# One transformer-like layer on one core: slicing the S5 outputs between projection tiles and reordering the attention heads

## The chip, the cores and the metric

The kernel runs on one core of one Trainium2 chip. TensorE (PE) does matrix products and transposes into eight PSUM banks, VectorE (DVE) and ScalarE (ACT) work on SBUF and PSUM, GpSimd (Pool) on SBUF alone, and SyncE (SP) issues most of the DMAs. The metric is device time in microseconds, from several runs, lower is better.

## The reference

One layer over 512 tokens of width 1024, batch 1, in float32, with a memory of 256 rows:

```
proj = rms_norm(h) @ w_in                # u_ssm, q, k, v: 512 columns each
y_ssm = s5_mixer(u_ssm, ...)             # 32 groups x 16 channels, 64 complex states, gelu, GLU
y_att = moba_attention(q, k, v, bias)    # 8 heads of 64; here plain causal attention with a T5 bias
h = h + concat(rms_norm(y_ssm), rms_norm(y_att)) @ w_out
h = h + memory_cross_attention(rms_norm(h), rms_norm(mem), ...)   # 4 heads of 128
h = h + conv_ffn(rms_norm(h), ...)       # width 2816, depthwise convolution of 3, silu gate
```

## The kernel before

Every engine has a program written out by hand, and its order is the order of the source; semaphores are the only tie between engines. A weight matrix is cut into units of 1024 columns per partition. Two units make a chunk of 1 MB, loaded by `load_chunk` (L451) into one of two `raw` buffers. ScalarE rounds a unit to fp32r in `split_hi` (L468), DVE takes the remainder in `split_lo` (L484), and both halves lie in a ring of four units, `wring`. A product is three matmuls, hi*hi, hi*lo and lo*hi (`mm3`, L503). A projection unit (`rows_unit`, L1713) goes over four token tiles with two steps of the depth, so it is 4 x 2 x 3 = 24 matmuls of 512 columns.

PSUM banks are handed out by `plan` (L268): `use(bank, name)` gives a name the next turn of a bank, `fill` (L343) makes TensorE wait until the earlier user of that bank is drained, and `drained` says that its last reader is done. So a name waits for the name that stands before it in the list of the same bank.

The S5 mixer runs in four quarters q of eight groups. TensorE transposes the input weights (`weights_in`), makes the input states (`states_in`, banks 4 and 5 as vr, vi) and the short kernels (`kernels_in`, banks 6 and 7 as ka, kb, laid out in Toeplitz form by eight DMAs in `t_load`, L599); DVE runs `scan(q)` (L1373) over vr, vi and drains them; TensorE then does `outputs(q)` (L1863), 24 small matmuls into banks 6 and 7 (ye, yo); ScalarE copies them out (`y_out`), SP carries them through DRAM (`y_back`, L611), and DVE adds the skip (`skip_in`). Between these steps stand the units of the q, k and v projections, 4 to 15. The PE order is at L1894 to L1916. `m_transposes` transposes the memory into banks 6, 7, 4, 5, read by ScalarE (`m_hi`) and drained by DVE (`m_lo`, L1363). `head_event` and `head_rows` are DVE's norms of q, k and mk per head; qt and kt are the transposed q and k, also in banks 6, 7, 4, 5. The roots of the row norms of x come from a pow on Pool and a correction of four steps on DVE (`root("x")`, L1207); TensorE needs them for the bank xb, behind the transposes cr and cm.

The attention runs over 32 steps s (four query tiles x eight heads): `scores(s)`, `logits(s)` on DVE, `probabilities(s)` (exp) on ScalarE, `prob_transposes(s)` into bank 6, `pt_evac(s)` in turns on ScalarE (even s, in its round s+1) and DVE (odd s, in its round s+1), `values(s)`. Scores use banks 3, 4, 5 in turn and are issued two steps ahead, first in a step. Other matrix work is laid between: memory keys (units 16 to 19) at `MK_AT`, GLU tiles at `GLU_AT`, memory values at `MV_AT`, the S5 half of the output projection in 16 pieces at `SOUT_AT`, whose inputs (the gated S5 result times its gain, hi part on ScalarE, lo part on DVE, strided) are made at s = 16 to 18. `SPLIT_AT` lays the splits over the steps. Behind the loop follow the attention half of the output projection, the memory attention and the feed-forward part, which take most of the time and are not changed but for the shape of the chunks of w_out.

Of the kernel before, what the change touches and what calls it, by code (L numbers as in the profile page):

```python
# [20 lines left out]
TT = T // 128  # L21
# [3 lines left out]
G, CG, NS = 32, 16, 64  # L25
GP = G // 2
# [28 lines left out]
U_SSM, U_Q, U_K, U_V, U_MK, U_GLU = 0, 4, 8, 12, 16, 20  # L55
U_MV, U_OUT, U_XQ, U_XO, U_UP, U_DOWN = 22, 26, 34, 38, 42, 86
# [13 lines left out]
SPLIT_AT = {2: 20, 4: 21, 6: 22, 8: 23, 11: 24, 13: 25, 15: 26, 17: 27, 19: 28, 21: 29, 30: 30, 31: 31}  # L70
YA_AT = [13, 23, 26]
# [27 lines left out]
def layer(nc, A, out):  # L99
# [10 lines left out]
    with ctx:  # L110
# [48 lines left out]
        turn_at = [region(at, GP, NC) for at in (R0 + 1152, R0 + 3328)]  # L159
# [36 lines left out]
        w1p = [region(at, 2, 512) for at in (R0 + 2304, R2 + 2048, R2 + 3072, R1 + 4096)]  # L196
        qT = region(R2, 4, T)
# [70 lines left out]
        def plan():  # L268
# [53 lines left out]
            for b in range(8):  # L322
# [6 lines left out]
                     U_GLU: "z1", U_GLU + 1: "z3", U_OUT + 1: "g30", U_OUT + 3: "g31",  # L329
                     U_OA + 1: "o30", U_OA + 3: "o31", U_XQ + 3: "qx3", U_XO + 1: "w30", U_XO + 3: "w31"})  # L330
# [69 lines left out]
        def chunk_src(c, r=0):  # L400
# [1816 lines left out]
```

## Time and profile before

| | |
|---|---|
| median of three runs (lowest, highest) | 746.7 us (744.6, 746.76) |
| the profiled execution | 746.4 us |
| its span, first to last instruction | 744.8 us |
| TensorE busy, share of the span | 97% |
| DVE, ScalarE, Pool busy | 57%, 42%, 15% |
| mean granted TensorE clock | 0.977 |

TensorE's busy time is modelled, so it says where the engine stood idle but not how fast it went; the granted clock is shown beside it, 1.00 being 2.4 GHz and 0.50 being 1.2 GHz. A line number can be that of a helper, so operations are told apart by their tiles: `pb` are the PSUM banks, `xs` and `bs` the inputs in two parts, `wring` the split weights, `F` one large buffer that holds nearly all else.

### The profile page before, as it was taken

To read this page: it belongs to the slowest core of one execution; us is meant where nothing else is said; L and a number is where in the kernel's file an instruction comes from. 1 tells how busy PE (TensorE), PEld (TensorE's weight loads), DVE (VectorE), ACT (ScalarE), POOL (GpSimd) and SP (SyncE) were. 2 spreads that over 40 slices of the span, in tenths; PEclk is the share of its full clock that TensorE was granted. 3 is DMA by queue.
4 is the path that set the end of the run, shared out by engine and by line. 5 is a ranking of instruction groups with operands and counts; after the bars stand their busy time and mean duration, and the time that the engine had idled before them with its cause. 6 is when DMAs were issued, how large, how long until landed. Compare 5 with 4: busy or idle time off the path is not lost.

```text
span 744.8 us, 10611 instructions
## 1 busy us (share of the span) xinstructions
PE 720.0 (97%) x3809; PEld 600.0 (81%) x3809; DVE 423.5 (57%) x718; ACT 312.1 (42%) x523; POOL 108.5 (15%) x114
## 2 busy tenths in 40 slices
PE   8798999988999999999999999999999999999998
PEld 8777888876777787787899888888888887888886
DVE  5989948144775445768586555555555474333322
ACT  5632746336674333535355434333343442323220
POOL 3889922004020000110010000000000000000000
PEclk9999999879998999999999999999999999999999
DMA  8637313266313003303031333233223213322302
GB/s 252 197 104 140 102 73 89 83 194 213 119 56 114 1 1 142 113 1 113 1 114 57 113 113 102 67 113 113 65 103 113 95 74 114 113 73 96 113 1 113
DMA packets 64022, 73.93 MB, mean 99 GB/s; under 512 B 20873, under 2 KB 47796, under 8 KB 63860
## 3 DMA queue, kind: packets, MB, share of 16 engines
q1 hardware_dynamic: 60196, 66.12, 27.6%
q10 hardware_dynamic: 3792, 7.36, 2.9%
q8 instruction: 21, 0.34, 0.2%
q14 instruction: 13, 0.11, 0.0%
HBM read 68.08 MB, written 5.78 MB: 99 GB/s over the span
## 4 chain that ended last, share of the span: by engine, by line
PE 87%; DVE 6%; ACT 3%; issue 2%; SPq 1%; DMA 1%; POOL 0%; ACTq 0%; DVEq 0%
PE pb L505 24%; PE pb L507 24%; PE pb L506 23%; PE pb L1690 11%; PE pb L1693 5%; DVE F L1189 2%; ACT F L833 1%; ACT xs L833 1%; DVE wring L491 1%; ACT wring L477 1%; DVE wring L488 1%; DVE xs L1195 1%; SPq L608 1%; ACT L833 1%; DVE F L1195 0%
## 5 line engine op out<-in xcount | busy, mean ns | idle before, releaser
L488 DVE TENSOR_TENSOR wring<-raw,wring 128x1024 fp32r<-128x1024 f32 x100 | 126.9, 1271 | 93.0 <-ACT wring L477 92.9
L505 PE MATMUL pb<-xs,wring 128*128 128x512 f32 (+1 forms) x448 | 166.0, 371 | 0.3 <-issue 0.2
L507 PE MATMUL pb<-xs,wring 128*128 128x512 f32 (+1 forms) x448 | 164.9, 368 | 0.0
L506 PE MATMUL pb<-xs,wring 128*128 128x512 f32 (+1 forms) x448 | 164.7, 368 | 0.0
L477 ACT ACTIVATE wring<-raw 128x1024 fp32r<-128x1024 f32 x100 | 105.2, 1055 | 105.0 <-PE pb L507 83.1
L1195 DVE SCALAR_TENSOR_TENSOR F<-pb,ccol,F 128x511 f32<-128x511 f32 x88 | 65.9, 749 | 103.3 <-ACT F L833 97.4
L505 PE MATMUL pb<-wring,bs 128*128 128x512 f32 x240 | 98.5, 410 | 0.9 <-DVE F L1195 0.5
L505 PEld LDWEIGHTS pb<-xs,wring 128*128 128x128 f32 x448 | 84.9, 190 | 14.8 <-issue 0.6
L506 PEld LDWEIGHTS pb<-xs,wring 128*128 128x128 f32 x448 | 84.9, 190 | 13.8
L507 PEld LDWEIGHTS pb<-xs,wring 128*128 128x128 f32 x448 | 84.8, 189 | 13.8
L507 PE MATMUL pb<-wring,bs 128*128 128x512 f32 x240 | 94.8, 395 | 0.0
L506 PE MATMUL pb<-wring,bs 128*128 128x512 f32 x240 | 94.7, 395 | 0.0
L1690 PE MATMUL pb<-F 128*128 128x64 f32 (+6 forms) x736 | 85.2, 290 | 3.4 <-DMA F<-F 2.4
L833 ACT ACTIVATE F<-pb,ccol 128x512 f32<-128x512 f32 x44 | 34.2, 778 | 121.4 <-PE pb L507 117.4
L505 PE MATMUL pb<-wring,xs 128*128 128x512 f32 x192 | 82.8, 431 | 1.4 <-DVE wring L491 0.9
L1690 PEld LDWEIGHTS pb<-F 128*128 128x128 f32 (+3 forms) x736 | 68.4, 175 | 9.8 <-DMA F<-F 2.9
L507 PE MATMUL pb<-wring,xs 128*128 128x512 f32 x192 | 76.1, 396 | 0.0
L506 PE MATMUL pb<-wring,xs 128*128 128x512 f32 x192 | 76.0, 396 | 0.0
L1693 PE MATMUL pb<-ident,F 128*128 128x128 f32 (+1 forms) x359 | 55.6, 282 | 11.7 <-ACT F L833 3.7
L1693 PEld LDWEIGHTS pb<-ident,F 128*128 128x128 f32 (+1 forms) x359 | 44.2, 145 | 25.1 <-issue 9.3
L505 PEld LDWEIGHTS pb<-wring,bs 128*128 128x128 f32 x240 | 46.1, 192 | 11.4 <-DVE F L1195 0.9
L507 PEld LDWEIGHTS pb<-wring,bs 128*128 128x128 f32 x240 | 45.8, 191 | 10.0
(138 smaller groups left out, 754.7 us busy)
## 6 DMA issues: line engine op xcount, KB each, us to landing
raw<-in_ffn_w_up SPq DMA_DIRECT2D x22, 1024.0 KB, 5.0
raw<-in_ffn_w_down SPq DMA_DIRECT2D x11, 1024.0 KB, 4.7
F<-in_x SPq DMA_DIRECT2D x8, 512.0 KB, 5.3
raw<-in_w_in ACTq DMA_DIRECT2D x4, 1024.0 KB, 5.7
raw<-in_w_out SPq DMA_DIRECT2D x4, 1024.0 KB, 5.0
raw<-in_w_in SPq DMA_DIRECT2D x3, 1024.0 KB, 6.3
raw<-in_x_wkv ACTq DMA_DIRECT2D x2, 1024.0 KB, 5.0
raw<-in_x_wkv SPq DMA_DIRECT2D x2, 1024.0 KB, 7.7
```

The costliest lines, as they stand in the source:

```text
L477: ins = nc.scalar.activation(w_unit(u, 0), raw_unit(u), ACT.Copy)
L488: ins = nc.vector.tensor_tensor(w_unit(u, 1), raw_unit(u), w_unit(u, 0).bitcast(f32), ALU.subtract)
L491: ins = nc.vector.scalar_tensor_tensor(out=w_unit(u, 1)[:, k, :], in0=raw_unit(u)[:, k, :], scalar=gcol[:, g + k:g + k + 1], in1=w_unit(u, ...
L505: nc.tensor.matmul(ps, lh, rh, start=first, stop=False)
L506: nc.tensor.matmul(ps, lh, rl_, start=False, stop=False)
L507: return nc.tensor.matmul(ps, ll, rh, start=False, stop=last)
L608: sync.dma_start(toep[d * CG:(d + 1) * CG, :, (L - 1 - d) * CG:], kt[0:CG, :, 0:(d + 1) * CG]).then_inc(t_in[q], 16)
L833: return nc.scalar.activation(o, i, f, **k)
L1189: return V.tensor_tensor(o, a, b, op)
L1195: return V.scalar_tensor_tensor(out=o, in0=a, scalar=s1, in1=b, op0=o1, op1=o2)
L1690: return nc.tensor.matmul(o, l, r, start=start, stop=stop)
L1693: return nc.tensor.transpose(o, i, ident[0:i.shape[0], 0:i.shape[0]])
```

## The change

The order of the programs on all engines is changed between the first projections and the end of the attention loop; the amount of matrix work stays.

- `rows_unit` becomes `rows_tile`, one token tile of a unit (six matmuls). `outputs(q)` becomes `outputs(q, a)`, a quarter of it. Slices of `outputs(0)`, `(1)`, `(2)` stand in turn with the tiles of units 8, 11, 14; those of `outputs(3)` with tiles of the last two memory key units, behind `scores(0)` and `scores(1)`.
- `kernels_in(q)` moves ahead of `states_in(q)` for q = 1, 2, 3, with `weights_in(q)`; two more projection units stand ahead of `m_transposes`. SP issues `t_load(q+1)` ahead of `y_back(q)`, and `scr_b` after the first.
- The memory keys move out of the head loop into the last S5 quarter. In the loop each step gets at most one tile of other work: memory values at s = 0 to 7, GLU at 8 to 11, output pieces at 14 to 30. Scores go to banks 3 and 4 only, behind the transposes of the step.
- The gated S5 parts are made one per step, on ScalarE at s = 11 to 14 and on DVE at s = 12 to 15. Chunks of w_out are two depth rows x 1024 columns.
- The correction of the roots of x moves from DVE to Pool, and DVE, ScalarE and SP are reordered to match.

The core of the diff (of the constants, the bank plan and each engine's order):

```diff
-U_SSM, U_Q, U_K, U_V, U_MK, U_GLU = 0, 4, 8, 12, 16, 20
-U_MV, U_OUT, U_XQ, U_XO, U_UP, U_DOWN = 22, 26, 34, 38, 42, 86
+U_SSM, U_Q, U_K, U_V, U_MK, U_MV = 0, 4, 8, 12, 16, 20
+U_GLU, U_OUT, U_XQ, U_XO, U_UP, U_DOWN = 24, 26, 34, 38, 42, 86
...
-MK_AT = [0, 2, 4, 6]
+MV_AT = [0, 1, 2, 3, 4, 5, 6, 7]
 GLU_AT = [8, 9, 10, 11]
-MV_AT = [12, 14, 16, 19]
+KX_AT = [5, 7]
+SS_AT = 17
-SOUT_AT = [23, 23, 24, 24, 25, 25, 26, 26, 27, 27, 28, 28, 29, 30, 31, 31]
+SOUT_AT = [14, 15, 16, 17, 18, 19, 21, 22, 23, 24, 25, 26, 27, 28, 29, 30]
+SOUT_ORDER = [(0, 1, 2, 3), (0, 2, 1, 3), (0, 2, 1, 3), (0, 2, 1, 3)]
+SOUT_DONE = [18, 19, 20, 23, 25, 27, 29, 31]
-SPLIT_AT = {2: 20, 4: 21, 6: 22, 8: 23, 11: 24, 13: 25, 15: 26, 17: 27, 19: 28, 21: 29, 30: 30, 31: 31}
-YA_AT = [13, 23, 26]
+SPLIT_AT = {0: 22, 1: 23, 2: 24, 4: 25, 11: 26, 12: 27, 13: 28, 15: 29, 28: 30, 30: 31}
+YA_AT = [12, 20, 26]
...
+                use(4, f"w1r{q}"); use(5, f"w1i{q}"); use(6, f"ka{q}"); use(7, f"kb{q}")
+                if q == 3:
+                    four("kt")
+                use(4, f"vr{q}"); use(5, f"vi{q}")
+                if q < 2:
+                    four(("m", "qt")[q])
                 use(6, f"ye{q}"); use(7, f"yo{q}")
             for s in range(TT * H):
-                use(3 + s % 3, f"sc{s}"); use(6, f"pt{s}")
+                use(3 + s % 2, f"sc{s}"); use(6, f"pt{s}")
...
@@ SyncE @@
+                t_load(q + 1)
                 y_back(q)
-                t_load(q + 1)
...
@@ Pool @@
             pow_event(EVN["x"])
+            pool.wait_ge(pow_ready, 1)
+            r, t, m = ev(rs, "x"), rt[:, 1, 0:TT], ev(ms, "x")
+            link(mul(t, r, r))
+            link(mul(t, t, m))
+            link(ts(t, t, -0.5, 1.5, ALU.mult, ALU.add))
+            mul(r, r, t).then_inc(xr_ready, 1)
...
+                if q == NQ - 1:
+                    pow_event(EVN["mk"])
...
@@ ScalarE @@
+            split_hi(act, 6)
             weights_in(0)
+            load_chunk(act, 4)
+            split_hi(act, 7)
+            kernels_in(0)
             act.wait_ge(turn_ready, 1)
             A_(ph[:, 1], turn_at[1], ACT.Sin, scale=-2 * math.pi)
...
             probabilities(0)
+            y_out(3)
+            act.wait_ge(mem_ready, 1)
+            mem_rows("mk", mkrow)
...
@@ DVE @@
             u_evac(2)
+            split_lo(dve, 5)
+            u_evac(3)
             turns(2)
-            u_evac(3)
+            split_lo(dve, 6)
             turns(3)
+            split_lo(dve, 7)
...
             scan(0)
+            split_lo(dve, 8)
+            split_lo(dve, 9)
+            head_event("q", qk, range(TT), H, "q")
+            m_lo()
+            split_lo(dve, 10)
+            head_rows("q", qk, range(TT), H, HD)
...
@@ TensorE @@
+            proj(4, U_Q, "q")
             weights_in(0)
+            proj(5, U_Q, "q")
+            states_in(0)
+            kernels_in(0)
+            proj(6, U_Q, "q")
+            proj(7, U_Q, "q")
             m_transposes()
+            for t in range(TT):
+                outputs(0, t)
+                proj_tile(8, U_K, "k", t)
             weights_in(1)
+            kernels_in(1)
             proj(9, U_K, "k")
+            states_in(1)
             proj(10, U_K, "k")
+            for t in range(TT):
+                head_transposes("qt", 0, qk, t)
+            for t in range(TT):
+                outputs(1, t)
+                proj_tile(11, U_K, "k", t)
             weights_in(2)
+            kernels_in(2)
             proj(12, U_V, "v")
+            states_in(2)
             proj(13, U_V, "v")
+            for t in range(TT):
+                outputs(2, t)
+                proj_tile(14, U_V, "v", t)
             weights_in(3)
+            kernels_in(3)
+            for t in range(TT):
+                proj_tile(15, U_V, "v", t)
+                if t < 2:
+                    head_transposes("kt", TT, qk, t)
+                elif t == 2:
+                    head_transposes("kt", TT, qk, 2)
+                    head_transposes("kt", TT, qk, 3)
+            states_in(3)
+            for n in range(4):
+                mem_tile(n, U_MK, "mk")
...
             scores(0)
             scores(1)
+            for a in range(QP):
+                outputs(3, a)
+                mem_tile(4 + a, U_MK, "mk")
```

## Rows read from the trace of the kernel before

**Rows 1.** The page: busy time of each engine, and the splits on DVE.

```profile
PE 720.0 (97%) x3809; PEld 600.0 (81%) x3809; DVE 423.5 (57%) x718; ACT 312.1 (42%) x523; POOL 108.5 (15%) x114
...
L488 DVE TENSOR_TENSOR wring<-raw,wring 128x1024 fp32r<-128x1024 f32 x100 | 126.9, 1271 | 93.0 <-ACT wring L477 92.9
```

**Rows 2.** Waits of TensorE, 0 to 300 us: total us, times, longest.

```profile
PE pb L1690 <- DVE rs L1189: 3.9, 1, 3.9
PE pb L1693 <- ACT F L833: 3.5, 3, 2.6
PE pb L1690 <- DMA F<-F: 2.4, 1, 2.4
PE pb L1693 <- DVE F L1189: 2.4, 1, 2.4
...
PE pb L1693 <- DVE F L379: 1.6, 1, 1.6
PE pb L1690 <- ACT F L833: 0.7, 1, 0.7
PE pb L505 <- DVE F L1195: 0.4, 1, 0.4
```

**Rows 3.** Busy by stretch: length, PE, PEld, DVE, ACT, POOL, clock, DMA share, GB/s.

```profile
102.81:107.50 4.69, 4.69 (x50) 4.15 (x49) 1.23 (x1) 2.94 (x5) 0.00 (x0) 1.00 0.04 15
107.50:110.91 3.41, 3.41 (x13) 3.02 (x14) 0.00 (x0) 1.86 (x4) 2.45 (x3) 0.50 0.21 77
131.39:141.63 10.24, 9.54 (x60) 8.54 (x61) 0.66 (x1) 3.57 (x7) 0.00 (x0) 0.67 0.22 84
155.03:168.94 13.91, 11.47 (x61) 10.05 (x62) 2.24 (x2) 4.52 (x8) 1.01 (x2) 0.63 0.75 212
...
223.55:230.38 6.83, 6.83 (x19) 5.26 (x20) 3.17 (x8) 1.62 (x3) 1.02 (x1) 0.50 0.46 157
```

**Rows 4.** Timeline of DVE (start, us), first step of the correction of x.

```profile
31.14 0.90 DVE L1189 TENSOR_TENSOR rt<-rs 128x4 f32<-128x4 f32 x1
```

**Rows 5.** Timeline of Pool (start, us): small steps and the pow of x.

```profile
13.93 0.22 POOL L707 TENSOR_TENSOR sp<-sp 128x16 f32<-128x16 f32 x1
14.24 1.16 POOL L721 TENSOR_SCALAR sp<-sp 128x16 f32<-128x16 f32 x1
...
28.99 1.88 POOL L755 TENSOR_TENSOR rs<-ms,mhalf 128x4 f32<-128x4 f32 x1 [2.91 <-DVE ms L1192]
```

**Rows 6.** Stretches: one scan on DVE; two projection units; three GLU heads.

```profile
56.51:62.55 6.04, 3.69 (x23) 2.98 (x22) 5.90 (x22) 0.00 (x0) 5.80 (x6) 1.00 0.43 81
...
84.34:95.52 11.18, 11.18 (x52) 9.22 (x51) 10.91 (x28) 6.11 (x8) 10.28 (x9) 1.00 0.36 90
...
191.60:203.16 11.56, 11.56 (x63) 9.75 (x61) 8.47 (x26) 5.84 (x16) 1.65 (x1) 1.00 0.25 92
```

**Rows 7.** Timeline of DVE: `m_lo`, two splits, two reductions.

```profile
67.18 3.23 DVE L1195 SCALAR_TENSOR_TENSOR bs<-pb,gcol,bs 128x256 fp32r<-128x256 f32 x8 [1.20 <-ACT bs L833]
70.32 3.74 DVE L488 TENSOR_TENSOR wring<-raw,wring 128x1024 fp32r<-128x1024 f32 x2
...
79.74 1.39 DVE L1235 TENSOR_REDUCE sq<-qz_odd 128x8 f32<-128x512 f32 x2
```

**Rows 8.** Timeline of ScalarE: the second Sin.

```profile
52.37 1.13 ACT L833 ACTIVATE F<-F,quart 128x1024 f32<-128x1024 f32 x1
```

**Rows 9.** Timeline of TensorE: the first matmuls of a unit behind small ones.

```profile
53.30 0.50 PE L505 MATMUL pb<-wring,xs 128*128 128x512 f32 x1
53.64 0.39 PE L506 MATMUL pb<-wring,xs 128*128 128x512 f32 x1
```

**Rows 10.** Timeline of ScalarE: tanh, split, two strided S5 parts.

```profile
195.44 0.68 ACT L833 ACTIVATE F<-pb,hbglu 128x512 f32<-128x512 f32 x1
...
214.14 1.05 ACT L477 ACTIVATE wring<-raw 128x1024 fp32r<-128x1024 f32 x1
...
215.64 2.27 ACT L833 ACTIVATE xs<-F,gcol 128x512 fp32r<-128x512 f32 x2
```

More of the change, by code:

```diff
@@ L885, in _ @@
                 drained(ins, name)
+            act.wait_ge(mem_in, 16 * MT)
+            for t in range(MT):
+                row_square(act, "mem", t, memr[:, t, :])
             split_hi(act, U_Q + 1)
@@ L921, in y_out, with rows @@
                             f"y{n}{q}")
-            def rows(name, dst):
-                for t in range(TT):
+            def rows(name, dst, tiles=range(TT)):
+                for t in tiles:
                     c = EVC["x"] + t
@@ L1480, in _ @@
             logits(0)
+            split_lo(dve, 21)
             for s in range(TT * H):
@@ L1894, in _, with head_transposes @@
+            def head_transposes(pre, base, src, t):
+                pe.wait_ge(xn_ready, base + t + 1)
+                p = fill(pe, f"{pre}{t}")
+                for a in range(4):
+                    last = tr(p[:, a * 128:(a + 1) * 128], src[:, t, a * 128:(a + 1) * 128])
+                filled(last, f"{pre}{t}")
+            proj(4, U_Q, "q")
             weights_in(0)
-            proj(4, U_Q, "q")
-            states(0)
             proj(5, U_Q, "q")
+            states_in(0)
+            kernels_in(0)
@@ L1909, in _ @@
+            for t in range(TT):
+                outputs(1, t)
+                proj_tile(11, U_K, "k", t)
             weights_in(2)
-            proj(11, U_K, "k")
-            states(2)
+            kernels_in(2)
             proj(12, U_V, "v")
+            states_in(2)
             proj(13, U_V, "v")
-            head_transposes("kt", TT, qk)
-            outputs(2)
+            for t in range(TT):
+                outputs(2, t)
+                proj_tile(14, U_V, "v", t)
             weights_in(3)
-            proj(14, U_V, "v")
@@ L1918, in _ @@
-            states(3)
-            proj(15, U_V, "v")
-            outputs(3)
+            kernels_in(3)
+            for t in range(TT):
+                proj_tile(15, U_V, "v", t)
[7 more added lines that the diff above has]
+                mem_tile(n, U_MK, "mk")
@@ L1961, in glu_tile, with piece @@
                 filled(last, f"z{m}")
-            def piece(t, i, u0, units, act_tile, name):
-                u, (half, j) = u0 + i, divmod(i, units)
+            def piece(t, u, j, half, units, act_tile, name):
                 if t == 0:
@@ L1978, in sout_piece @@
             def sout_piece(n):
-                piece(n // 4, n % 4, U_OUT, 2, x_tile, lambda t, half: f"g{t}{half}")
+                t = n // 4
+                i = SOUT_ORDER[t][n % 4]
+                if t == 0:
+                    pe.wait_ge(ym_ready, 4 if i >= 2 else 2)
+                piece(t, U_OUT + i, i // 2, i % 2, 2, x_tile, lambda t, half: f"g{t}{half}")
             def tile_transposes(name, src):
```

338 lines of the change are left out of this document (145 added, 193 removed).

## Prediction

> **What bounds the kernel now.** The first lines of the page say that TensorE is busy 720.0 of 744.8 us [rows 1], and its chain is 87% TensorE, so the order is: where does TensorE stand idle, and where does it run at half clock. The profiled execution took 746.4 us, 1.6 around its span; the median of the three runs is 746.7, so I work from 746.4 and take 0.3% (about 2.2 us) as what can be told from no change. The waits of TensorE up to 300 us [rows 2], without the first DMA, are 3.9 for the reciprocal roots of x (`root("x")` on DVE), 2.4 for `scan(0)` (banks 4 and 5, in `m_transposes`), 0.7 and 2.4 around `outputs(2)` and `outputs(3)`, 3.5 at the first heads, 1.6 at head 18, 0.4 behind the loop: 15.0. The stretches by clock [rows 3] are the second loss. After each of these places the granted clock is at 1.2 instead of 2.4 GHz: once with no wait before it (102.81 to 107.50 is `outputs(1)`, TensorE busy throughout, and the next 3.41 us have 0.50). Missing clock times length: 3.41 x 0.5 = 1.7, and two more like it behind the waits of 3.9 and 2.4 (from 35.8 and 63.1); 10.24 x 0.33 = 3.4; 13.91 x 0.37 = 5.1; 6.83 x 0.5 = 3.4. Together 17.0. The change touches nothing but these regions, so **at most 15.0 + 17.0 = 32.0 us** can go, to 714.4.
>
> **What is removed.** The matrix work is the same. *x root on Pool*: `mean_sq("x")` moves ahead of `turn_step`, to about 26.5 instead of 28.7, and four small Pool operations follow the pow, 1.88 in before. Pool's small steps take 0.22, one in some ten 1.16 [rows 5]; with 0.1 between them, 1.3 to 2.3. The roots stand at 29.8 to 30.8, TensorE asks at 30.6: 3.9 becomes 0 to 0.2. DVE loses a chain that began with 0.90 for four elements while Pool worked [rows 4], 3.3 us in all. *Projections between*: `scan(0)` gets two more units before `m_transposes`, so 2.4 goes; each quarter of `outputs` stands ahead of one projection tile, so 0.7 and the low clock around the outputs go; `t_load(3)` is issued some 10 us ahead of its use, so 2.4 goes. *Heads*: the memory keys, two banks for scores, and scores after the transposes take away the 3.5; the sums of S5 are spread, which takes the 1.6 with its 3.4 of clock; the 0.4 goes as `split_lo(31)` is inside the loop.
>
> **What is late next.** I walked every engine's queue in the new order with the durations of before. A projection unit is 5.6 (11.18 for two [rows 6]), a tile 1.4, a `scan` 6.0 [rows 6].
> 1. *u3's bank*: `split_lo(5)` is now ahead of `u_evac(3)`. Projection 4 starts at 38.4 and reaches its last tile at 42.5; the evacuation ends at 43.2. +0.7.
> 2. *`outputs(0)` behind `m_lo`*. It fills banks 6 and 7, last used by m0 and m1, which DVE drains in `m_lo`. TensorE: 38.4 + four units 22.4 + weights 0.9 + states and kernels 3.0 + m 1.9 + 0.7 = 67.2. ScalarE issues Sin only behind the copies of `kernels_in(0)` (TensorE at 54.1, copied 55.1), and two Sin of 1.1 [rows 8] end at 57.3. Then DVE: scan 6.0, splits 8 and 9 3.7, four reductions of 0.7, the mean 0.5, four of the eight parts of `m_lo` 1.6 [rows 6, 7]: 71.9. A wait of 4.7, and as after the shorter wait of before a low clock: 1.7 for one stretch, 3.4 for two; I take 2.5. +7.2. If Pool (busy throughout) slowed DVE less, splits take 1.2 instead of 1.9 (the mean of all 100 is 1.27 [rows 1]) and the wait is 1.
> 3. *`outputs(1)` behind the copies of qt0 and qt1*, same banks: four copies of 0.6 against transposes that TensorE does in 2.0. +0.9.
> 4. *`outputs(2)` behind `scan(2)`*: one unit of cover, 5.6, for 6.0 and a DVE that is late by 0.9. +1.4. `scores(1)` behind `scan(3)`: +0.4.
> 5. *Heads 2 to 4*: DVE has `head_event("mk")` and `head_rows("mk")` there, 2.9 and 2.0 as at heads 8 and 10 of before, but with heads of 2.1 in place of 3.9 (11.56 for three [rows 6]). Probability bank 6 is single, so transposes of s wait until those of s-1 are copied. +2.7.
> 6. *Heads 12 to 16*. Between heads 11 and 13 ScalarE gets three splits (1.05), three strided parts of S5 (1.1), two tanh (0.7) and three squares (0.6), ya square and copy 1.1, exps and copies 1.9 [rows 10]: about 12 us issued back to back. TensorE has 3.8 + 1.4 + 1.0, since heads 12 and 13 have no tile. The copy of head 12's transposes is ScalarE's first step in round 13, so transposes 13 wait 3.2. DVE has two splits, two strided parts (1.1 each here too), two gatings, `ya_lo`: its copy of head 13 comes 13.8 after the start of head 11, TensorE is there at 10.8: 3.0. Then the third S5 piece waits 0.5 for `ym_ready` 4, and behind it in TensorE's queue stand transposes 16 and scores 18, which DVE and ScalarE need next. +6.7, and 0 to 3.4 of clock, I take 1.5: +8.2.
> 7. *Changes of kind of work*. From small matmuls to a unit the first step is 0.34 instead of 0.23 [rows 9]; about 24 more round trips (twelve in the outputs, three with kt, nine in heads). Back and forth at 0.1 to 0.2: 2.4 to 4.8, I take 3.0; below nothing is excluded since the same instructions run.
>
> *Moved queues*: `pow_event` of mk now stands on Pool ahead of the last GLU input, which waits with it for DVE's means (near 171); head 8 needs it 15 us later. `t_load(1)` now holds SP until `kernels_in(1)` is copied (87), and `y_back(0)`, whose reader is `skip_in(0)` at 102, is done at 102; `scr_b` moves ahead and its 8.2 us have 40 us of cover; the bias read still waits for `scan(3)` and lands near 161, about when DVE has finished split 20. If it is later, all heads are: +1 for 1.
>
> Sum: 746.4 - 32.0 + 0.2 + 0.7 + 7.2 + 0.9 + 1.8 + 2.7 + 8.2 + 3.0 = **739.1**.
>
> **Rows against the Trainium skill.** Pool's small multiply took 0.22 [rows 5], DVE's on four elements 0.90 [rows 4]. The Trainium skill (GPSIMD Engine Reference, section 4.1) says not to put elementwise work there, two-input operations being about twice as slow. By it the move would cost 3.3 more instead of saving; the row decides and the sum goes by it. On the clock, [rows 3] show a fall behind a stretch that was busy. The Trainium skill (TensorE: Matmul & The Clock Gate, What's actually happening) ties half rate to idleness; by it slicing would bring nothing at `outputs(1)`, 1.7 less.
>
> **Rivals.**
> A. *The new waits don't come*, because DVE is not slowed where Pool now pauses and ScalarE runs ahead at the heads. For it: DVE has idle time in before from 100 on. Against: the queues of points 2 and 6 have no gap to give. 746.4 - 32.0 + 0.2 + 0.7 + 0.9 + 1.8 + 3.0 = 721.0, with a wait of 1 at point 2 722. Chance 0.17.
> B. *The waits come back one for one*: points 2, 5 and 6 half as large again (9 more) through Pool's sums beside DVE and a low clock after each wait. 748. Chance 0.12.
> C. *The clock stays low over the slices*, where TensorE changes banks and kind every 1.2 us. Four quarters of 4.7 + 5.6 are 41 us. At 1.2 GHz throughout 739.1 + 20.5 = 759.6, in two of the four 749.4; it decides (slower than 748.9) from 20 of the 41. Against: heads at 191.60 to 203.16 alternate alike and have 1.00 [rows 6]. The Trainium skill (TensorE: Matmul & The Clock Gate, A second HAM failure mode) tells of a kernel that changes banks and whose clock swings; that is this rival. Chance 0.11.
> D. *x root on Pool does not do what it says*: with steps of 1.16 each [rows 5] behind the pow the roots stand at 33.4, a wait of 2.8 in place of 0.2 and a low clock return: 739.1 + 2.6 + 1.7 = 743.4. Chance 0.08.
> The forecast, with errors of a third on points 2 and 6, is 731 to 746, chance 0.52.
>
> **Numbers.** Likeliest 739.1. The range reaches into A and up to B: 723 to 749. Faster than 744.5: forecast 0.50, A 0.17, D 0.07, = 0.74. Within 0.3%: the upper edge, half of B, 0.13. Slower: C and the rest of B, 0.13.
>
> **What would show it.** No wait near 30.6 and no low clock behind it; a wait of 4 to 5 on DVE ahead of the first output slice, with a low clock behind; clock 1.00 in the slices (C wrong) or 0.50 (C right); no DMA wait ahead of `outputs(3)`; waits of about 3 each for the copies (DVE L379's counterpart and ScalarE's) at heads 13 and 14. If TensorE waits under 3 us in all between 60 and 220, points 2 and 6 are wrong and A holds.

## The result and the profile after

The changed kernel is slower: a median of 749.9 us in six runs (748.71 to 751.8) against 745.5 (743.96 to 746.76), a ratio of 1.0062 with a 95% interval of 1.004 to 1.0083. The forecast was 739.1 with a range of 723 to 749, so the median lies above the range and the sign is wrong. The profiled execution took 751.8 us, with a span of 750.2 and a mean clock of 0.979 (before: 746.4, 744.8 and 0.977). I follow its 5.4 us.

The first lines of the page, and the row of the splits, answer [rows 1]:

```profile
PE 718.2 (96%) x3809; PEld 596.8 (80%) x3809; DVE 417.4 (56%) x714; ACT 311.6 (42%) x523; POOL 113.1 (15%) x118
...
L488 DVE TENSOR_TENSOR wring<-raw,wring 128x1024 fp32r<-128x1024 f32 x100 | 128.2, 1284 | 80.2 <-ACT wring L477 80.1
```

TensorE is busy 1.8 us less in a span that is 5.4 longer: it waits more. The waits of TensorE from 0 to 300 us, as [rows 2] (total, times, longest):

```profile
PE pb L1700 <- DVE bs L1208: 5.9, 1, 5.9
PE pb L1703 <- DVE F L382: 5.4, 5, 1.7
PE pb L1703 <- ACT F L845: 2.7, 1, 2.7
PE pb L1703 <- DMA F<-in_norm_mix: 2.5, 1, 2.5
PE pb L505 <- ACT F L845: 2.4, 1, 2.4
PE pb L1700 <- POOL rs L683: 1.9, 1, 1.9
PE pb L505 <- DVE F L1208: 1.8, 1, 1.8
PE pb L1700 <- ACT qz_odd L845: 1.4, 1, 1.4
PE pb L1700 <- DVE F L1202: 0.7, 1, 0.7
```

Without the first DMA (`in_norm_mix`) these are 22.2 us, where before had 15.0. Of the list of before, the waits for `scan(0)`, for the DMA ahead of `outputs(3)`, for ScalarE at the first heads and at head 18 are gone as foreseen. Of the nine rows above, the first DMA and the roots of x (`rs`, now from Pool) are waits of before, and the last out piece (1.8, L1208) had 0.4; the others stand at new places. Their places, from TensorE's timeline (start, us, the wait in brackets):

```profile
32.55 1.16 PE L1700 MATMUL pb<-ident,rs 128*128 128x128 f32 x8 [1.91 <-POOL rs L683]
...
74.13 2.14 PE L1700 MATMUL pb<-F 128*128 128x64 f32 x12 [5.91 <-DVE bs L1208]
...
105.58 1.22 PE L1700 MATMUL pb<-F 128*128 128x64 f32 x12 [1.35 <-ACT qz_odd L845]
124.36 0.60 PE L505 MATMUL pb<-wring,xs 128*128 128x512 f32 x1 [2.44 <-ACT F L845]
...
184.72 0.30 PE L1703 MATMUL pb<-ident,F 128*128 128x128 f32 x1 [1.67 <-DVE F L382]
...
217.48 0.66 PE L1703 MATMUL pb<-ident,F 128*128 128x128 f32 x2 [2.67 <-ACT F L845]
224.13 0.66 PE L1703 MATMUL pb<-ident,F 128*128 128x128 f32 x2 [1.72 <-DVE F L382]
...
286.49 0.47 PE L505 MATMUL pb<-wring,xs 128*128 128x512 f32 x1 [1.77 <-DVE F L1208]
```

The stretches at low clock, as [rows 3] (length, busy time of PE, PEld, DVE, ACT, POOL, clock, DMA share, GB/s), with one at full clock, the slices of `outputs(2)`, as the last row but one:

```profile
72.89:79.72 6.83, 5.59 (x22) 4.77 (x22) 6.69 (x13) 2.75 (x5) 6.16 (x5) 0.53 0.46 154
...
107.03:113.86 6.83, 6.83 (x27) 5.55 (x26) 1.23 (x1) 1.67 (x3) 0.00 (x0) 0.53 0.59 151
124.09:127.50 3.41, 3.14 (x8) 2.50 (x9) 2.06 (x3) 3.41 (x7) 1.96 (x2) 0.57 1.01 342
139.15:149.50 10.35, 10.35 (x73) 8.72 (x74) 5.93 (x10) 1.07 (x3) 0.00 (x0) 1.00 0.33 103
216.25:229.90 13.65, 10.70 (x31) 8.18 (x32) 10.56 (x16) 8.53 (x17) 4.41 (x3) 0.52 0.23 77
```

Each low stretch starts in or just behind one of the waits above. (The windows are cut within 0.1 to 0.2 us of the steps of the clock, hence 0.53 and not 0.50.) Together 30.7 us of low clock, so 15.4 of missing clock time; before had 34.1, so 17.0. The 5.4 us are then: waits +7.2, clock -1.7, about 0 for everything else. This execution is the slowest of the six, and by its low clock above their median.

For all kernels below I split the time of every run in the same way, because the place of the low stretches varies from run to run: **missing clock time** is the span times (1 - mean clock), and **full-clock time** is the rest of the span, which holds work and waits. The clock is given to a thousandth, so each is good to 0.4 us. The kernels were measured in several sets of runs, each with its own runs of before. The median of before was between 745.4 and 746.9 us in them, and its full-clock time, in the four sets of the experiments, between 727.6 and 728.1. So differences of medians between kernels are good to some 2 us, those of full-clock time to half a microsecond; the intervals given with each experiment compare with before in the same set. The columns are medians, each by itself, so they need not add up to the median time.

| kernel | median us | runs | full-clock time | missing clock time |
|---|---|---|---|---|
| before (with the first experiments) | 746.2 | 25 | 728.1 | 17.1 |
| after | 749.9 | 6 | 735.5 | 13.5 |
| e1, `m_lo` first | 743.9 | 10 | 733.4 | 9.6 |
| e2, three splits moved | 744.1 | 10 | 733.8 | 8.9 |
| e3, projection tile first at `outputs(1)` | 747.8 | 10 | 733.3 | 12.7 |
| e4, k rows ahead of the kernels | 746.4 | 10 | 734.7 | 10.4 |
| e6, last out piece first | 747.8 | 10 | 733.6 | 13.4 |
| e5, root of x back on DVE | 757.1 | 4 | 736.9 | 17.3 |
| e8, outputs unsliced | 756.6 | 4 | 735.5 | 19.6 |
| e7, all of e1 to e6 | 738.9 | 6 | 729.7 | 7.0 |
| e9, e1 to e4 and e6 | 730.9 | 5 | 726.8 | 1.5 |
| e10, e9 and tile first in all three | 726.9 | 5 | 725.1 | 0.0 |
| e12, e10 with the outputs unsliced | 733.5 | 6 | 723.8 | 8.0 |
| e11, before with the root of x on Pool | 747.6 | 12 | 727.7 | 17.2 |

By the medians, too, the change gained clock (17.1 to 13.5) and paid with waits (728.1 to 735.5).

### The profile page after: what moved, and what is told of

It reads as the page before. It is cut to its first block, busy times and chain, and to the rows that moved or that the text cites. A ratio compares the mean times of both kernels' runs of the same rounds, so it can differ in the third digit from the quotient of the medians.

```text
span 750.2 us, 10610 instructions
## 1 busy us (share of the span) xinstructions
PE 718.2 (96%) x3809; PEld 596.8 (80%) x3809; DVE 417.4 (56%) x714; ACT 311.6 (42%) x523; POOL 113.1 (15%) x118
## 4 chain that ended last, share of the span: by engine, by line
PE 85%; DVE 8%; ACT 3%; issue 2%; POOL 1%; DMA 0%; ACTq 0%; DVEq 0%; POOLq 0%
PE pb L505 24%; PE pb L507 23%; PE pb L506 23%; PE pb L1700 11%; PE pb L1703 4%; DVE F L1202 2%; DVE wring L488 2%; ACT F L845 1%; ACT xs L845 1%; DVE sq L1248 1%; DVE wring L491 1%; DVE pb L1202 1%; DVE xs L1208 1%; DVE F L1208 0%; ACT wring L477 0%
## 5 line engine op out<-in xcount | busy, mean ns | idle before, releaser
L1208 DVE SCALAR_TENSOR_TENSOR F<-pb,ccol,F 128x511 f32<-128x511 f32 x88 | 65.9, 749 | 103.4 <-ACT F L845 97.5
L505 PE MATMUL pb<-wring,bs 128*128 128x512 f32 x240 | 96.4, 402 | 0.9 <-DVE F L1208 0.5
L506 PEld LDWEIGHTS pb<-xs,wring 128*128 128x128 f32 x448 | 84.5, 189 | 13.5
L507 PE MATMUL pb<-wring,bs 128*128 128x512 f32 x240 | 93.7, 390 | 0.0
L506 PE MATMUL pb<-wring,bs 128*128 128x512 f32 x240 | 93.5, 390 | 0.0
L1700 PE MATMUL pb<-F 128*128 128x64 f32 (+6 forms) x736 | 83.2, 285 | 8.2 <-DVE bs L1208 5.9
L1700 PEld LDWEIGHTS pb<-F 128*128 128x128 f32 (+3 forms) x736 | 71.7, 172 | 22.0 <-issue 15.6
L505 PE MATMUL pb<-wring,xs 128*128 128x512 f32 x192 | 83.9, 437 | 5.1 <-ACT F L845 2.4
L507 PE MATMUL pb<-wring,xs 128*128 128x512 f32 x192 | 78.1, 407 | 0.0
L506 PE MATMUL pb<-wring,xs 128*128 128x512 f32 x192 | 77.8, 405 | 0.0
L1703 PEld LDWEIGHTS pb<-ident,F 128*128 128x128 f32 (+1 forms) x359 | 43.3, 143 | 23.9 <-issue 13.7
L505 PEld LDWEIGHTS pb<-wring,bs 128*128 128x128 f32 x240 | 45.1, 188 | 10.9 <-DVE F L1208 0.9
L507 PEld LDWEIGHTS pb<-wring,bs 128*128 128x128 f32 x240 | 45.0, 188 | 9.7
```

The source lines that it names most:

```text
L505: nc.tensor.matmul(ps, lh, rh, start=first, stop=False)
L506: nc.tensor.matmul(ps, lh, rl_, start=False, stop=False)
L507: return nc.tensor.matmul(ps, ll, rh, start=False, stop=last)
L1208: return V.scalar_tensor_tensor(out=o, in0=a, scalar=s1, in1=b, op0=o1, op1=o2)
L1700: return nc.tensor.matmul(o, l, r, start=start, stop=stop)
L1703: return nc.tensor.transpose(o, i, ident[0:i.shape[0], 0:i.shape[0]])
```

## The experiments

My theory behind the result: six places of the new order, each of them a queue in which a piece of work stands one or two steps too early, make TensorE wait, and the low clock comes back behind the waits. The rivals: the slices themselves are too weak work to hold the clock (then only undoing them helps), or the waits move elsewhere when one is removed. Edits are against the changed kernel unless said.

**e1, the largest wait.** In DVE's order:

```diff
-            head_event("q", qk, range(TT), H, "q")
             m_lo()
+            head_event("q", qk, range(TT), H, "q")
```

> The changed kernel with m_lo ahead of head_event(q) on DVE. Theory (the wait ahead of the first output slice is DVE's queue): m_hi ends at 70.7 in the changed kernel and its second part at about 68.8, so m0 and m1 are drained near 69.5 to 70 instead of 74; the wait of 5.9 falls to 1.2 to 2, the low clock behind it from 6.8 us to 0 to 3.4. Total 4 to 7 us less than the changed kernel (about 743 to 746), since nothing else is tight until the qt copies. Rival (DVE is the bound of this whole stretch, so what is done first only moves the wait): the four reductions come later, the q norms with them, and the wait comes back at the qt transposes; total within 1 us of the changed kernel.

743.9 us (742.04 to 749.28), ratio to before 0.998, interval 0.9952 to 1.0007: 6.0 less than the changed kernel. In the profiled run the wait of 5.9 became 2.2, at 70.07, and the stretch that had 0.53 before now has 1.00:

```profile
70.07 1.22 PE L1700 MATMUL pb<-F 128*128 128x64 f32 x12 [2.22 <-DVE bs L1208]
...
72.89:79.72 6.83, 6.83 (x51) 5.78 (x51) 5.91 (x10) 3.35 (x6) 5.79 (x5) 1.00 0.44 151
```

**e2, heads 12 to 16.** Three splits leave the crowded heads:

```diff
-SPLIT_AT = {0: 22, 1: 23, 2: 24, 4: 25, 11: 26, 12: 27, 13: 28, 15: 29, 28: 30, 30: 31}
+SPLIT_AT = {0: 22, 1: 23, 2: 24, 4: 25, 7: 26, 9: 27, 10: 28, 15: 29, 28: 30, 30: 31}
```

> The changed kernel with the splits of units 26, 27, 28 at steps 7, 9, 10 instead of 11, 12, 13. Theory (heads 12 to 16 wait for ScalarE and DVE, which get twelve us of work against six): three us leave ScalarE and DVE there; waits of 2.7 and 1.7 at heads 13 and 14 fall to about 1 and 0, the low clock of 13.7 us behind them goes at least by half; total 4 to 8 us less. Rival (the strided S5 parts alone are enough, each 1.2 on both engines, one behind the other): waits fall by under 1 us in all, the low clock stays, total 0 to 2 us less.

744.06 us (741.46 to 745.16), ratio 0.9959, interval 0.9937 to 0.998: 5.8 less. Its stretch over the same heads, and the waits from 180 to 250:

```profile
215.78:229.43 13.65, 11.62 (x62) 9.15 (x63) 10.35 (x21) 9.45 (x21) 5.33 (x3) 1.00 0.13 39
...
PE pb L1703 <- DVE F L382: 4.5, 5, 1.7
PE pb L1703 <- ACT F L845: 1.7, 1, 1.7
```

The waits fell by only 1.9 (8.1 to 6.2), less than I had expected, but the 13.65 us of low clock are gone: TensorE did 62 matmuls here where it did 31 in 216.25 to 229.90 of the changed kernel. The size of this is in part chance: with the waits of these heads untouched, the profiled runs of e1, e4, e6 and e8 have 6.8 us of low clock here and those of e3 and e5 13.7. But in none of the five kernels with the splits moved is there any.

**e3, a projection tile ahead of the slice, at `outputs(1)`.**

```diff
             for t in range(TT):
-                outputs(1, t)
                 proj_tile(11, U_K, "k", t)
+                outputs(1, t)
```

> The changed kernel, in the second quarter alone each projection tile ahead of its output slice. Theory (the low clock of 6.8 us in these slices came from the wait of 1.35 for the qt copies together with weak work): the tile covers the wait, the stretch has clock 1.00, total 1.35 + 3.2 = about 4 us less. Rival (the slices alone are too weak for the clock): the wait goes, but the clock still falls to 0.50 for 3.4 us or more in that stretch, total 1 to 2 us less.

747.8 us (745.12 to 749.56), ratio 1.0013, interval 0.9991 to 1.0034: 2.1 less. The wait for the copy of qt1 is gone, and so is the low clock of this quarter, with the slices still there:

```profile
105.80:117.00 11.20, 11.20 (x82) 9.36 (x81) 3.29 (x4) 5.32 (x10) 0.00 (x0) 1.00 0.51 147
```

So the slices alone do not bring the low clock. That the wait of 1.35 brings it is not shown: e4 and e5 have the same wait ahead of the same slices and ran through them at full clock (the row under e4), e1, e2 and e6 were low there for 3.4 us, the changed kernel for 6.83. Over ten runs the missing clock time is only 0.8 less than that of the changed kernel (12.7 and 13.5), and less came back than the 4 expected.

**e4, the bank of v0.** In ScalarE's order:

```diff
             weights_in(2)
+            rows("k", qk, range(2))
             kernels_in(2)
-            rows("k", qk)
+            rows("k", qk, range(2, TT))
```

> Edit: ScalarE copies the k rows of the first two tiles ahead of the kernels of the third quarter, not behind them. In the changed kernel TensorE waits 2.4 us at 124.36 for ScalarE's copy of k0 and runs 3.41 us at half clock from 124.1, which costs 1.7. Theory (the copies stand behind the kernels in ScalarE's order, and the bank of v0 waits for k0's): the wait of 2.4 goes and the 1.7 of clock with it, and the kernels of the third quarter come some 2 us later, for which outputs(2) may wait up to 1: 746 to 748, as a median. Rival (k0's copy is late for a cause of its own, such as the products that it copies): the wait stays over 1.5 and the time stays within 1 us of the changed kernel, 749 to 751.

746.38 us (744.38 to 748.87), ratio 1.0, interval 0.9979 to 1.0021: 3.5 less. The wait of 2.44 is 0.19 now (first row), and the clock from 124 to 127.4 is 1.00. The second row is the stretch at `outputs(1)`, from the start of its wait of 1.35 on, at full clock:

```profile
121.39 0.47 PE L505 MATMUL pb<-wring,xs 128*128 128x512 f32 x1 [0.19 <-ACT F L845]
...
106.60:119.00 12.40, 11.04 (x79) 9.44 (x80) 3.02 (x3) 5.13 (x10) 1.23 (x2) 1.00 0.43 132
```

The clock in one profiled run is weak evidence by itself: in those of e5 and e8 the wait of 2.44 stands as before, and the clock behind it is 1.00 too.

**e5, the root of x back on DVE** (with the mean still first): the four steps leave Pool, and in DVE's order

```diff
             split_lo(dve, 3)
+            root("x", xr_ready)
             dve.wait_ge(pw_ready, 1)
```

> Edit: the four small steps that refine the root of x stand on VectorE again, behind the fourth low half of x; the first mean comes before them, as in the changed kernel. Theory (Pool's small steps take 1.04 to 1.17 us each beside VectorE's wide ones, so that the transpose of x at 32.55 waits 1.9 us): that wait falls to under 1.0, since VectorE ends the fourth low half by about 31.2 and does the four steps in about 0.5; no stretch of low clock hangs on it in the changed kernel, so about 1 us is saved: 748.5 to 750. Rival (the wait is for x's low half or the mean that stands before the root): it stays at 1.9 or grows, 750 to 751.

757.06 us (754.3 to 757.29), ratio 1.0137, interval 1.0105 to 1.017: 7.2 *slower* than the changed kernel (some 5.8 when each is set against before in its own set of runs). Theory and rival both missed. TensorE waits 1.5 instead of 1.9 for the roots, and a new wait of 3.93 stands at 44.52, ahead of the first q projection, for DVE's evacuation of the first banks:

```profile
44.52 0.77 PE L505 MATMUL pb<-wring,xs 128*128 128x512 f32 x1 [3.93 <-DVE F L1196]
```

I had given DVE's four steps 0.5 us. They took 3.4, and one reason stands in the two timelines of this kernel, DVE's above, Pool's below:

```profile
29.30 1.02 DVE L1196 TENSOR_TENSOR rt<-rs 128x4 f32<-128x4 f32 x1
30.36 0.98 DVE L1196 TENSOR_TENSOR rt<-rt,ms 128x4 f32<-128x4 f32 x1
31.38 0.17 DVE L1199 TENSOR_SCALAR rt<-rt 128x4 f32<-128x4 f32 x1
31.58 1.11 DVE L1196 TENSOR_TENSOR rs<-rs,rt 128x4 f32<-128x4 f32 x1
```

```profile
28.16 3.16 POOL L683 TENSOR_TENSOR F<-pw,F 128x512 f32<-128x512 f32 x2
31.40 1.27 POOL L689 TENSOR_TENSOR F<-F 128x512 f32<-128x512 f32 x1
```

DVE's second and fourth step end at 31.34 and 32.69, Pool's wide steps at 31.32 and 32.67. The third, of 0.17, started at 31.38, in the gap between two of Pool's steps (31.32 to 31.40). That it has only one input is not what spared it: another such step on 128 x 2 elements, at 41.55 in this kernel, took 1.12 and ended at 42.67, Pool's wide step at 42.65. In the changed kernel the roles are swapped: there Pool has the small steps and DVE the wide ones (Pool's timeline above, DVE's below):

```profile
27.80 1.17 POOL L683 TENSOR_TENSOR rt<-rs 128x4 f32<-128x4 f32 x1
29.05 1.06 POOL L683 TENSOR_TENSOR rt<-rt,ms 128x4 f32<-128x4 f32 x1
30.20 1.04 POOL L713 TENSOR_SCALAR rt<-rt 128x4 f32<-128x4 f32 x1
31.32 1.17 POOL L683 TENSOR_TENSOR rs<-rs,rt 128x4 f32<-128x4 f32 x1
```

```profile
27.68 1.22 DVE L488 TENSOR_TENSOR wring<-raw,wring 128x1024 fp32r<-128x1024 f32 x1
28.83 2.35 DVE L1202 TENSOR_TENSOR F<-sp,kidx 128x1024 f32<-128x1024 f32 x2
31.21 1.22 DVE L1202 TENSOR_TENSOR F<-F 128x1024 f32<-128x1024 f32 x1
```

Here Pool's steps end at 28.97, 30.11, 31.24 and 32.49, the DVE steps at 28.90, about 30.0 (half of the x2 row), 31.18 and 32.43. In both kernels a step of four elements, once it meets a wide step of the other engine, lasts until that is over. What differs is who loses: DVE's wide steps keep their 1.2 in the changed kernel, and DVE's queue is the one that TensorE waits for. The Trainium skill (SBUF — State Buffer, Who interferes with whom) says that a DVE instruction with two SBUF inputs contends with a Pool instruction that reads SBUF, that the shared pair of ports is an exclusive lock, and that the order of issue decides who is blocked. The ends in these four timelines agree.

The four steps are not the whole delay. DVE's evacuation of the first bank starts at 42.59 here and at 37.15 in the changed kernel, 5.4 later: 0.5 was there before the steps, they added 3.3, and the wide DVE steps behind them, which now run beside Pool's wide ones, took 1.7 longer (the first three 3.21 and 1.97, in the changed kernel 2.35 and 1.22).

**e6, the last out piece.** At the end of the heads, in DVE's order:

```diff
+            residual("g31", TT - 1, 1, rs[:, EVC["ss"] + TT - 1:EVC["ss"] + TT])
             normalise(f"pv{TT - 1}", H * (TT - 1), H, HD, TT - 1)
             split_lo(dve, U_OA + 2)
-            residual("g31", TT - 1, 1, rs[:, EVC["ss"] + TT - 1:EVC["ss"] + TT])
```

> Edit: at the end of the heads VectorE writes the last out piece of the first token tile before it normalises the last head and before the low half of unit 32, not behind them. In the changed kernel TensorE waits 1.8 us at 286.49 for this piece, whose bank the next out piece takes. Theory (the bank is wanted at once since pieces alternate halves, and VectorE's order holds it): the wait falls to 0.5 or less, while the low half of unit 32 comes 0.6 us later and is not waited for: 748 to 749. Rival (the same wait moves to the normalised head or to unit 32's low half): the sum of waits between 280 and 300 stays at 1.8, and the time at 749.9.

747.79 us (746.59 to 750.76), ratio 1.002, interval 1.0001 to 1.0039: 2.1 less. The wait is 0.24, now for the low half of unit 32. The gain is work and waits (733.6 against 735.5), not clock.

**e8, the slices undone.** All four `outputs` in one stretch each, with the projection behind them, the rest of the new order kept:

```diff
             for t in range(TT):
                 outputs(0, t)
-                proj_tile(8, U_K, "k", t)
+            proj(8, U_K, "k")
```

and so for the other three quarters.

> The changed kernel with outputs(q) whole again, ahead of its projection or memory unit (all four quarters). Theory (slicing is worth what it does for the clock): waits stay, the low clock grows by one stretch of 3.4 to 6.8 us at the third and the fourth quarter, where the changed kernel has none: 3.5 to 7 us more (about 753 to 757). Rival (slicing costs as much in changes between kinds of work as it saves): the same within 1 us; at 0.1 to 0.2 for each of 12 round trips 1.2 to 2.4 less than the theory.

756.56 us (755.55 to 757.95), ratio 1.0142, interval 1.01 to 1.0183: 6.7 more than the changed kernel (6.0 by the two sets of runs with before). Its waits from 60 to 175 are the same four (5.9, 2.4, 1.4, 0.7) and its full-clock time is the same 735.5; all that is lost is clock, with no overlap between the runs: 18.8 to 20.4 us missing in four, 10.5 to 15.8 in the six of the changed kernel.

**e7, all six edits together.**

> Edit: all six together: the low halves of the first kernel ahead of the rotation of q, three low halves of later units moved from heads 11 to 13 to heads 7, 9 and 10, the projection tile ahead of the output slice in the second quarter, the k rows ahead of the kernels of the third quarter, the root of x back on VectorE, the last out piece first. Theory (the lateness of the changed kernel is these six waits and the low clock behind them, each removable by itself): waits of TensorE from 0 to 300 fall from 22.2 to about 10, low clock from 30.7 to 7 to 14 us in length: 749.9 - 12 - 9 = 729, range 727 to 736; faster than the kernel before by 1.5 to 2.5%. Rival (the clock's low stretches move elsewhere when some are taken away, as when the splits' edit left 13.7 us of low clock at the first slices): waits fall, but 20 us or more of low clock stay: 737 to 742.

738.88 us (735.5 to 741.97), ratio 0.9885, interval 0.9852 to 0.9919. Below both kernels, but short of the 729 that I expected: the root on DVE brings its wait with it here as well (5.2 at 45.22, and 1.5 at 32.23), and a low clock of 6.8 us that begins inside the wait. Its profiled run has 10.2 us more of low clock at the first outputs, behind the wait of 2.2 that e1 had left there; in the profiled run of e1 there was none behind the same wait.

**e9, without the root.**

> Edit: the six edits together, without the one that puts the root of x back on VectorE. Theory (each wait can be taken out by itself, and the root on Pool is worth its place): against the kernel of all six the waits for VectorE at 45 (5.2) and at the roots of x (1.5 in place of Pool's 1.9) go, 4.8 less: 738.9 - 4.8 = 734.1, and a low clock behind the wait at 45 goes with it, 1.7 to 3.4 more, when no other stretch takes its place: 731 to 735. Rival (the low clock returns elsewhere as waits go): missing clock stays at 7 and the time at 735 to 737.

730.92 us (729.6 to 732.12), ratio 0.9812, interval 0.9786 to 0.9837, lower than I expected. The five edits alone gave 6.0 + 5.8 + 2.1 + 3.5 + 2.1 = 19.5 less than the changed kernel, together they give 19.0. Set against before in each set of runs the five come to 24.5 and the whole to 18.9, so that the total adds up is shown only roughly. The full-clock time does add up: 2.1 + 1.7 + 2.2 + 0.8 + 1.9 = 8.7, and 8.7 together; a wait of 0.86 for a low half at 293.39 is new. The gain is 8.7 of full-clock time, nearly all waits, and 12.0 of clock.

The profiled runs say where the clock was low (length in us at each place; "slices" are those of the outputs, and v0 is the wait of 2.44):

| kernel | first slices | slices of `outputs(1)` | v0 | heads 12 to 16 | elsewhere |
|---|---|---|---|---|---|
| after | 6.8 | 6.8 | 3.4 | 13.7 | |
| e1 | 0 | 3.4 | 3.4 | 6.8 | |
| e2 | 13.7 | 3.4 | 3.4 | 0 | |
| e3 | 13.7 | 0 | 3.4 | 13.7 | |
| e4 | 13.7 | 0 | 0 | 6.8 | |
| e5 | 10.2 | 0 | 0 | 13.7 | 6.8 at 42 |
| e6 | 6.8 | 3.4 | 3.4 | 6.8 | |
| e8, unsliced | 13.7 | 10.2 | 0 | 6.8 | 6.8 at `outputs(2)` |
| e7 | 10.2 | 0 | 0 | 0 | 6.8 at 43 |
| e9 | 0 | 0 | 0 | 0 | 3.4 at 12.5 |

Where a cause was left alone, the length still changes from one kernel to the next, at `outputs(1)` and v0 down to nothing. So one place in one profiled run does not show what a wait costs. What holds in every row is that the long wait at the first slices (5.0 to 5.9) and the crowded heads, wherever they are left in, had a low clock.

**e10, the tile first in the first and third quarter as well.**

```diff
-                outputs(0, t)
                 proj_tile(8, U_K, "k", t)
+                outputs(0, t)
```

> Edit: the kernel before this in the list, with the projection tile ahead of the output slice in the first and the third quarter too. Theory (a tile of 1.4 ahead of the first slice covers what is left of these waits): 2.2 becomes 0.8 at outputs(0), 0.7 becomes 0 at outputs(2), and less low clock behind the first: 2 to 4 us less than the kernel of five edits, 728 to 732. Rival (the slices end a tile later in each quarter, so the copies of the outputs, the next states and the scans are late by up to 1.4): 0 to 1 less.

726.91 us (726.53 to 728.16), ratio to before 0.9758, interval 0.9733 to 0.9784: 4.0 less than e9, a little more than expected. **It beats both kernels**: 2.4% under before, about 3% under the changed one. The mean clock of the profiled run is 0.999. The two largest waits of TensorE that are left behind the start (the others are 1.6 at the roots of x, 0.9 for a low half, 0.8 at `outputs(0)` and smaller ones), and the stretch of the heads:

```profile
PE pb L1704 <- DVE F L382: 4.4, 5, 1.7
...
PE pb L1704 <- ACT F L845: 1.7, 1, 1.7
...
200.00:240.00 40.00, 38.60 (x217) 30.64 (x218) 22.39 (x55) 17.05 (x42) 5.93 (x4) 1.00 0.08 27
```

**e12, e10 with the outputs in one stretch.** The first projection tile, then all four slices, then the other three tiles; in the last quarter the four slices, then the memory tiles. The waits are those of e10.

> Edit: the kernel with a projection tile ahead of every quarter, but the four slices of each quarter in one stretch of 4.7 us, behind the first projection tile, the other three tiles behind them; waits as there. It tells whether the slices or the waits hold the clock. Theory (both do: 4.7 us of small matmuls alone bring a low clock even without a wait, as at 102.81 to 107.50 of before): low clock of 3.4 to 6.8 us behind two to four of the quarters, 4 to 10 us of time lost, waits the same: 731 to 737. Rival (with the waits gone the clock stays at full speed over whole quarters too): 727 to 728.

733.49 us (730.6 to 735.54), ratio 0.9831, interval 0.9801 to 0.9861: 6.6 more than e10 (6.0 by the two sets of runs with before), all in the clock. 3.6 to 11.0 us of it are missing in six runs, 0.0 to 1.5 in the five of e10. Two whole outputs and what follows them:

```profile
72.78:77.54 4.76, 4.76 (x49) 4.22 (x49) 4.62 (x9) 2.50 (x3) 4.60 (x5) 1.00 0.01 3
77.91:81.32 3.41, 3.41 (x10) 2.68 (x9) 2.56 (x6) 3.06 (x6) 2.24 (x2) 0.52 0.63 174
101.69:105.22 3.53, 3.53 (x37) 3.12 (x36) 1.13 (x2) 3.12 (x5) 0.00 (x0) 0.98 1.02 320
105.22:112.04 6.82, 6.82 (x25) 5.58 (x24) 0.84 (x1) 0.66 (x2) 3.65 (x3) 0.51 0.31 65
```

TensorE has no gap in any of the four rows, and the clock falls behind (or in) the stretch of small matmuls, as in [rows 3] at 107.50. The other two outputs, at 130.84 and 157.55, ran on at 1.00, and a third low stretch of 3.4 us, at 33.5, stands behind the wait for the roots of x and not behind outputs. So slices and waits both decide: with neither fault next to no clock is missing. The Trainium skill (TensorE: Matmul & The Clock Gate, What's actually happening) has half rate follow idleness; by that alone the whole outputs of e12 would have cost nothing, and its rows show 3.41 and 6.82 us at half clock behind them without a gap.

The stretch from 70 to 160 us of four kernels, in the order e8, after, e12, e10, shows both in one view:

```profile
70.00:160.00 90.00, 80.55 (x518) 66.58 (x519) 42.42 (x89) 33.32 (x56) 31.29 (x26) 0.83 0.29 83
```
```profile
70.00:160.00 90.00, 81.33 (x558) 66.74 (x560) 41.15 (x89) 36.59 (x59) 30.53 (x25) 0.91 0.32 87
```
```profile
70.00:160.00 90.00, 88.88 (x643) 72.72 (x642) 55.72 (x113) 44.68 (x73) 34.34 (x26) 0.94 0.41 110
```
```profile
70.00:160.00 90.00, 88.93 (x674) 73.63 (x675) 60.63 (x116) 45.59 (x72) 37.99 (x29) 1.00 0.46 128
```

Whole outputs with the waits: busy 80.55, clock 0.83. Sliced with the waits: 0.91. Whole without the waits: busy 88.88, 0.94. Sliced without: 1.00, and 674 matmuls in 90 us instead of 518.

**e11, the root on Pool alone, in the kernel before.** The four steps behind the pow on Pool, the mean first on DVE, `root("x")` taken out; all else as before.

> Edit: the kernel before with this part of the change alone: the mean of x first on VectorE, and the four steps behind the power on Pool. Theory (this part is a gain by itself: VectorE's steps beside Pool's wide ones took 3.3 us and Pool's take some 4.8 but start 2 us sooner, and VectorE goes on): the wait of 3.9 for the roots falls to 1.9, and of the two low stretches around 36 and 63 the first goes in most runs: 746.5 - 2.0 - 1.7 = 742.8, range 742 to 745. Rival (Pool's wide steps for the first kernels come 4 us later, and states or kernels wait for them): the time stays within 1 us of before, 745.5 to 747.5.

747.58 us (745.22 to 750.13), ratio 1.002, interval 1.0 to 1.0041. The rival was the nearer: nothing is gained (before had 745.37 in this set of runs, so it is 2.2 slower, more than the 1 that the rival allowed). The roots come 1.5 us sooner, and then

```profile
32.98 1.16 PE L1695 MATMUL pb<-ident,rs 128*128 128x128 f32 x8 [1.75 <-POOL rs L680]
...
54.15 3.60 PE L1695 MATMUL pb<-F 64*16 64x128 f32 x32 [5.29 <-POOL F L794]
```

the kernels of the first quarter wait 5.3 us for Pool, whose queue is longer by the four steps; the wait of 2.4 for `scan(0)` behind them is gone in return. In the changed kernel another projection unit stands ahead of these kernels, and there is no such wait. The part is a gain only in company.

## Why the prediction was wrong

The sum was 746.4 - 32.0 + 24.7 = 739.1. Of the 24.7, 17.7 were waits, 4.0 clock, 3.0 changes of kind of work. The trace has 22.2, 15.3 and 0: 746.4 - 32.0 + 22.2 + 15.3 = 751.9, against 751.8 measured. This counts all that is left as new; by place not all of the 32.0 went, since the roots of x still cost 1.9 of their 3.9, and at `outputs(1)` the clock is still low, for 6.83 us in place of 3.41. The errors are +4.5 in the waits, -3.0 in the changes of kind and, **by far the largest, +11.3 in the clock** (by the medians of the table 13.5 are missing where 4.0 were forecast: +9.5).

- *The clock behind the new waits* is the step that failed. I had put 2.5 behind `m_lo`, 1.5 at the heads and nothing elsewhere. There were 3.4 at 72.9, 3.4 at 107.0, 1.7 at 124.1 and 6.8 at 216.3 (half the length of each low stretch). I had read in [rows 3] that the clock falls beside work of small matmuls even without a wait, and still priced it as a by-product of long waits only. What the runs show in its place: behind the wait at the first slices, while it was 5.0 to 5.9, the clock was low for 6.8 to 13.7 us in all seven profiled kernels that have it, so 3.4 to 6.8 of time against 2.5; at heads 12 to 16 for 6.8 or 13.7 in all seven with the splits at 11 to 13, so 3.4 to 6.8 against 1.5, and for nothing in the five with the splits moved; and at `outputs(1)` and v0, where I had put nothing, in most. Five edits to the queues gave back 12.0 us of it.
- *Point 2, `outputs(0)` behind `m_lo`*: mechanism right, 4.7 foreseen, 5.91 measured. The second Sin ended at 58.45, not at 57.3, two splits took 4.29 and not 3.7, the mean 0.89 and not 0.5; TensorE asked at 68.2, not at 67.2. DVE was not faster, as rival A would have had it.
- *Point 3, copies of qt*: 0.9 foreseen, 1.35 measured; its clock (3.4) was missing.
- *Point 4*: 1.8 foreseen, 0.7 measured; `scores(1)` has no wait.
- *Point 5, heads 2 to 4*: 2.7 foreseen, 1.67 + 0.83 = 2.5 measured.
- *Point 6, heads 12 to 16*: waits of 3.2, 3.0 and 0.5 foreseen; 0.56, 2.67, 1.72 and 0.61 measured. The place, the engines and the crowd of splits were right, as e2 shows; the clock there was 6.8 in this run, not 1.5.
- *Point 1, u3's bank*: 0.7 foreseen, none. TensorE reached the first q projection at 40.35 and not at 38.4, since the transposes of x had waited 1.7 longer than foreseen; that may have hidden it, and no run tests it.
- *Root of x*: 0.2 foreseen, 1.91 measured. This is rival D: each small step of Pool took 1.04 to 1.17. Its low clock did not come in this run (it did in e12's, at 33.5). That the part is worth keeping here is nevertheless so (e5), for a reason larger than the one I named: what it takes from DVE's queue, wide steps included.
- *Missed altogether*: 2.4 for the bank of v0, because ScalarE's k rows went behind `kernels_in(2)` (the change moved the kernels up, and I walked DVE's queue here but not ScalarE's); and 1.8 for the last out piece instead of a gain of 0.4: the out pieces now alternate between the halves, so the second of them wants the bank of g31 at once.
- *Point 7, changes of kind of work*: 3.0 foreseen; 0 in the trace of after. e8 and after have the same full-clock time (735.5), e10 has 1.3 more than e12. So slicing costs 0 to 1.3 us, which the spread between sets of runs does not let me tell more closely.
- *Rival C* is refuted: `outputs(2)` in slices ran at 1.00 (139.15 to 149.50), and in e9 and e10 all slices did. *Rival B* (waits and clock come back one for one) was the nearest by its number, 748; I had given it 0.12. Its account is right only for point 2 and for the clock at 2 and 6: points 5 and 6 waited no longer than foreseen, and behind 5 the clock did not fall.

What the change is for is sound: the slicing alone is worth 6 to 7 us in the changed kernel (e8) and again in the mended one (e12). Its gain was spent in five places of the queues, which e9 mends.

## What to carry to other kernels

Price a new wait of TensorE with the clock behind it, above all where the work around it is small matmuls: here five edits that removed 8.7 us of waits gave 12.0 us of clock on top. Take that price from many runs: the same wait of 2.44 had 3.4 us of low clock behind it in five profiled kernels and none in two. Long stretches of small matmuls are worth cutting up between large ones even if nothing waits, and the cutting is nearly free. When work is moved up in one engine's order, walk the order of every engine for what it now stands ahead of, and put a piece of large work in front of the first consumer, so that a short lateness is covered.

## What was not expected of the hardware

- Steps of 128 x 4 elements on Pool took 1.04 to 1.17 us each beside DVE's wide steps with two inputs, and 0.22 elsewhere [rows 5]. The same steps on DVE took 0.98 to 1.11 beside Pool's wide steps, and 0.17 where one fell into a gap between them. The engine with the small steps loses its time: DVE's wide steps kept their 1.2 beside Pool's small ones. Wide beside wide they took 1.6 to 2.1 (e5).
- The clock was low for 6.83 us behind a wait of 1.35 in a stretch of slices, for 3.4 behind the same wait in three other kernels, and not at all in e4 and e5. It stayed at 1.00 over heads in which waits of 1.7 and 0.8 remain (e10). e12 missed 8.0 us of clock time, and there is no gap around its two outputs behind which the clock fell. What exactly of a stretch decides remains open; no run here varied the size of the matmuls alone.
- The low stretches are not in the same places in every run: the missing clock time of e1 ranges from 6.7 to 15.7 in ten runs of one program, while its full-clock time stays within 731.5 to 734.5.
